# Loads of h spread over slots, first tiles' transposes and first copies moved ahead, dense stream of the forward GLA pass one unit ahead

## The reference

```
h = rmsnorm(x) * norm_g
proj = h @ w_in            # q,k,v and decay gates of the GLA, three z, q,k,v of the attention, cross q, merge gates
o_a = gla_branch(...) * silu(z_a)         # forward and backward scan over the tokens, summed
o_b = diff_attention(...) * silu(z_b);  o_c = memory_cross_attention(...) * silu(z_c)
merged = sum_i sigmoid(gate_i) * (o_i @ w_branch_i)
y = rmsnorm(x + merged @ w_out)
```

## Time and profile before

| | |
|---|---|
| median of three runs | 3385.5 us (3385.05 to 3393.41) |
| profiled execution | 3387.87 us, its span 3386.1 us |
| TensorE busy | 3268.4 us, 97% of the span |
| VectorE, ScalarE, GpSimd busy | 59%, 39%, 32% |
| DMA | 164 GB/s over the span |
| mean granted TensorE clock | 0.985 |

### The profile page before, as it was taken

The page is one execution under the profiler, slowest core; times in us unless marked ns, Lnnn a source line. Parts: engine busy times, 40 slices in busy tenths (PEclk is TensorE's granted clock), DMA queues, the critical chain, the costliest instruction groups (busy, mean ns, idle before and its releaser), DMA issues. The chain is left out here.

```text
span 3386.1 us, 50920 instructions
## 1 busy us (share of the span) xinstructions
PE 3268.4 (97%) x19012; PEld 2552.1 (75%) x19012; DVE 2010.2 (59%) x4623; ACT 1329.7 (39%) x2170; POOL 1097.9 (32%) x511
## 2 busy tenths in 40 slices
PE   7999999998999999999999988999999888999998
PEld 6888888887888888888877765666666566888887
DVE  3322312226667666676667778888888466556654
ACT  3111111114334343444322336666666565333322
POOL 2412313243333333333333325555555433000000
PEclk9999999999999999999999989999999999999999
DMA  6545445465454544544459964122121366667562
GB/s 210 191 147 185 166 153 182 167 216 182 135 191 138 186 149 132 193 137 148 138 168 298 323 209 146 38 78 77 53 63 38 106 236 220 235 225 240 174 219 73
DMA packets 319013, 555.62 MB, mean 164 GB/s; under 512 B 35694, under 2 KB 115438, under 8 KB 318768
## 3 DMA queue, kind: packets, MB, share of 16 engines
q1 hardware_dynamic: 267296, 471.66, 42.9%
q10 hardware_dynamic: 51472, 80.71, 6.6%
HBM read 382.43 MB, written 169.82 MB: 163 GB/s over the span
## 5 line engine op out<-in xcount | busy, mean ns | idle before, releaser
L774 POOL TENSOR_TENSOR glaf_w_lo<-early_raw,glaf_w_hi 128x1024 fp32r<-128x1024 f32 x140 | 342.9, 2450 | 631.0 <-ACT glaf_w_hi L748 629.4
L803 PE MATMUL glaf_dense_acc<-h_hi,glaf_w_hi 128*128 128x512 f32 x1120 | 451.3, 403 | 5.5 <-ACT glaf_dense_out L757 4.1
L803 PE MATMUL glaf_dense_acc<-h_lo,glaf_w_hi 128*128 128x512 f32 x1120 | 439.3, 392 | 0.0
L803 PE MATMUL glaf_dense_acc<-h_hi,glaf_w_lo 128*128 128x512 f32 x1120 | 436.5, 391 | 0.0
L1792 DVE CUSTOM_DVE_ANT_0 front_p<-diff_s_ps,ahead_table 128x512 f32<-128x512 f32 x544 | 347.2, 687 | 72.4 <-PE diff_s_ps L1654 71.6
L555 POOL TENSOR_TENSOR proj_w_lo<-early_raw,proj_w_hi 128x1024 fp32r<-128x1024 f32 x84 | 202.8, 2415 | 481.7 <-DVE proj_w_hi L505 481.7
L1735 ACT ACTIVATE front_p<-front_p,diff_neg_max 128x2048 f32<-128x2048 f32 (+1 forms) x160 | 278.8, 1743 | 7.1 <-DVE diff_neg_max L1800 7.0
L1678 PE MATMUL diff_oT_ps<-diff_aT,diff_v 128*128 128x512 f32 x544 | 272.4, 602 | 4.7 <-ACT diff_aT L1729 4.7
L215 PE MATMUL proj_acc<-h_hi,proj_w_hi 128*128 128x512 f32 x672 | 263.0, 391 | 0.6 <-POOL proj_w_lo L555 0.6
L1653 PE MATMUL diff_s_ps<-ahead_k,ahead_q_high 128*128 128x512 f32 x544 | 244.6, 450 | 18.4 <-PEq L75 8.7
L217 PE MATMUL proj_acc<-h_hi,proj_w_lo 128*128 128x512 f32 x672 | 261.7, 389 | 0.0
(11 more groups left out here) (223 smaller groups left out, 7158.8 us busy)
## 6 DMA issues: line engine op xcount, KB each, us to landing
early_raw<-in_w_zg SPq DMA_DIRECT2D x180, 512.0 KB, 4.2
early_raw<-in_w_stream SPq DMA_DIRECT2D x80, 512.0 KB, 3.6
scratch_zg<-glaf_dense_out SPq DMA_DIRECT2D x140, 256.0 KB, 2.2
items_raw<-in_w_br SPq DMA_DIRECT2D x120, 256.0 KB, 2.9
merge_gate<-scratch_zg SPq DMA_DIRECT2D x120, 256.0 KB, 3.4
scratch_featT<-proj_out ACTq DMA_DIRECT2D x80, 256.0 KB, 2.3
items_br_hi<-scratch_item_hi SPq DMA_DIRECT2D x60, 256.0 KB, 6.1
items_br_lo<-scratch_item_lo SPq DMA_DIRECT2D x60, 256.0 KB, 6.4
```

Of the source, the lines that this page charges most:

```text
L774: pool.tensor_tensor(self.w_lo[:, s], self.raw[:, u % self.RAW], self.w_hi[:, s], ALU.subtract).then_inc(self.lo_split, 1)
L803: done = pe.matmul(self.acc[:, u % self.banks], a, x, start=i == 0, stop=i == self.PER - 1)
```

## The change

Four edits, three of them in the order of instructions and one in the order of DMAs:

- Projection: the transposes of tile 1 stand inside `first_product`, ahead of its low-h matmuls; those of tiles 2 and 3 behind units 0 and 1 instead of 1 and 2. `high(1)` stands ahead of `high_resident(5)`, `high(2)` and `high(3)` behind the copies of units 0 and 1.
- Forward pass: 30 dense matmuls instead of 40 stand ahead of the first sums. `sums` is cast on ScalarE instead of VectorE, and unit 0 is copied out ahead of the first tile's exponentials instead of among them.
- Forward pass: from slot 6 of tile 0 on, `targets` is 24 higher (at most the total). Slot 6 of tile 0 so has 42 matmuls instead of 18, and the last tile's last two slots have none (18 and 6 before).
- Both passes: `load_h` issues one k per slot over eight slots in the forward pass, two per slot over four in the backward, instead of all eight at once. The loads at the start of the forward pass stay in one piece.

```diff
@@ phase_project, ScalarE and TensorE
             high_resident(4)
+            high(1)
             high_resident(5)
...
                 if c == 0 and at < TT - 1:
-                    high(1 + at)
+                    if 2 + at < TT:
+                        high(2 + at)
...
+                transpose(1)
                 pe.wait_ge(lo_ready, 1)
...
-                if c == 0 and at < TT - 1:
-                    transpose(1 + at)
+                if c == 0 and 2 + at < TT:
+                    transpose(2 + at)
@@ Dense
-    def load_h(self, sp, index):
+    def load_h(self, sp, index, pieces):
...
-        if index >= self.buffers:
+        if index >= self.buffers and 0 in pieces:
             sp.wait_ge(self.unit_done, self.first_of[index - self.buffers + 1])
-        for k in range(KT):
+        for k in pieces:
...
-            if u + 1 in self.first_of:
-                index = self.first_of.index(u + 1) - 1 + self.buffers
-                if index < len(self.chunks):
-                    self.load_h(sp, index)
+        for index in range(self.buffers, len(self.chunks)):
+            last = self.first_of[index - self.buffers + 1] - 1
+            first = (slot - [last in ended for ended in self.ended].index(True)) * self.pieces
+            if 0 <= first < KT:
+                self.load_h(sp, index, range(first, first + self.pieces))
@@ phase_gla_forward (pieces=1; phase_gla_backward passes pieces=2)
-        PER, FIRST_PRODUCTS = len(SHARES), 3
+        PER, FIRST_PRODUCTS = len(SHARES), 2
+        AHEAD_FROM, TOTAL = X_SLOTS, len(FORWARD_UNITS) * Dense.PER
+        targets = [t if i < AHEAD_FROM else min(t + Dense.PER, TOTAL) for i, t in enumerate(spread_over(TOTAL, SHARES, N))]
...
+            act.wait_ge(sums_in, 16)
+            act.activation(sums[:, :, :], sums_raw, ACT.Copy).then_inc(sums_ready, 1)
+            dense.copies(act, FIRST_PRODUCTS)
             for j in range(N):
...
-                        dense.copies(act, slot + 1 + d * PAIRS + a)
+                        if slot + 1 + d * PAIRS + a != FIRST_PRODUCTS:
+                            dense.copies(act, slot + 1 + d * PAIRS + a)
...
-            dve.wait_ge(sums_in, 16)
-            dve.tensor_copy(sums[:, :, :], sums_raw).then_inc(sums_ready, 1)
```

More of the change, by code:

```diff
@@ L673, with __init__ @@
     RAW, WEIGHTS, OUTS, PER = Early.RAW, 3, 2, 3 * KT
-    def __init__(self, m, h, early, which, held, hT_hi, hT_lo, w_zg, zg, units, targets, silu, banks):
+    def __init__(self, m, h, early, which, held, hT_hi, hT_lo, w_zg, zg, units, targets, silu, banks, pieces):
         self.dram = hT_hi, hT_lo, w_zg, zg
@@ L678, in __init__ @@
         self.units, self.count, self.buffers, self.targets, self.silu = units, len(units), H_BUFFERS, targets, silu
-        self.held = held
+        self.held, self.pieces = held, pieces
         self.chunks = list(dict.fromkeys(c for c, _ in units))
@@ L725, in begin_transfers @@
         for index in range(self.held, self.buffers):
-            self.load_h(sp, index)
+            self.load_h(sp, index, range(KT))
     def transfers(self, sp, slot):
@@ L828, in phase_gla_forward @@
         SHARES = [10] * X_SLOTS + [18, 30, 18, 18, 18, 6]
-        PER, FIRST_PRODUCTS = len(SHARES), 3
-        dense = Dense(m, h, early, 0, 1, hT_hi, hT_lo, w_zg, zg, FORWARD_UNITS, spread_over(len(FORWARD_UNITS) * Dense.PER, SHARES, N), False, 2)
+        PER, FIRST_PRODUCTS = len(SHARES), 2
+        AHEAD_FROM, TOTAL = X_SLOTS, len(FORWARD_UNITS) * Dense.PER
+        targets = [t if i < AHEAD_FROM else min(t + Dense.PER, TOTAL) for i, t in enumerate(spread_over(TOTAL, SHARES, N))]
+        dense = Dense(m, h, early, 0, 1, hT_hi, hT_lo, w_zg, zg, FORWARD_UNITS, targets, False, 2, 1)
         qk = m.sb("qk", [P, S, 4, P])
@@ L1200, in phase_gla_backward @@
         order = list(range(SEQS[0] // P - 1, -1, -1)) + list(range(N - 1, SEQS[0] // P - 1, -1))
-        dense = Dense(m, h, early, 1, 2, hT_hi, hT_lo, w_zg, zg, BACKWARD_UNITS, spread_over(len(BACKWARD_UNITS) * Dense.PER, [1, 1], N), True, 3)
+        dense = Dense(m, h, early, 1, 2, hT_hi, hT_lo, w_zg, zg, BACKWARD_UNITS, spread_over(len(BACKWARD_UNITS) * Dense.PER, [1, 1], N), True, 3, 2)
         qb = m.sb("qb", [P, L, PAIRS, P])
```

## The result

The changed kernel takes 3363.87 us (median of 4 runs, 3362.45 to 3367.64) where the kernel before, in turn with it on the same chip, takes 3387.51 (3385.05 to 3393.41): the ratio is 0.993, with a 95% interval of 0.9918 to 0.9943. It is 23.6 us faster, and 3362 was forecast. The total agrees; its terms agree less well.

The account below looks back on a forecast made before the run. TensorE was taken as the bound, full in mid forward pass, so only its waits could be won. Terms 9.3 + 8.1 + 1.0 + 0.4 + 5.0 = 23.8 us off 3387.87 give 3364.1; 2.4 lower for the median: 3362, range 3356 to 3371.

Parts of the forecast that it names:

- Projection: Projection: earlier transposes leave one wait of some 1.8 us and bring unit 3's copy to 46.3 from 55.85; 9.3 us.
- if all stays warm: Upper bound of the projection term, with no matmuls at the low clock: 10.3 us.
- Start of the forward pass: Forward pass start: waits of 4.07 and 1.67 us shrink or go, 24 matmuls are issued earlier; 8.1 us (7.3 to 8.7).
- The step that timed VectorE's chain: Forward pass start: VectorE's chain starts 2.2 us earlier and would be done at 800.0.
- h spread in the forward pass: Forward pass: the one wait for `w_lo`, after a block of 16 h DMAs, goes; 1.0 us (0 to 1.0).
- End of the forward pass: Forward pass end: `o_ps` starts 3.25 us later, but backward weights are issued earlier; 0.4 us gained (-1 to +1).
- h spread in the backward pass: Backward pass: `w_lo` waits of 2.58 and 0.6 us and 2.7 of cold matmuls shrink; 5.0 us (0 to 6.2).
- One sign that I had named against this term: Backward pass: the prediction would be wrong if ScalarE's waits for raw weights grew instead of shrinking.
- The rival that the backward waits stay: Backward pass: waits stay or move as the DMA queue hardly drains; term 0 to 1, total 3366 us, chance 0.20.
- that of a late clock: Projection: inserted transposes make the clock rise later; price 3.3 us, total 3365 us, chance 0.10.
- That of the margins at the forward start: Forward pass start: unit 1's copy comes too late and unit 3 stands; 2 to 4 us, total 3365, chance 0.08.
- It does nothing: Projection's wait only moves to tile 3, forward start's credit is all paid at its end; total 3377 us, chance 0.04.

Follow-up runs that it names:

- e7: The changed kernel with the projection edit undone (transposes and high parts back at their old places): 3373.72 us, ratio 0.9966 to the kernel before.
- e4: The changed kernel with the forward pass's dense stream not a unit ahead (old targets): 3361.01 us, ratio 0.993 to the kernel before.
- e2: The changed kernel with the loads of h in one block again in both passes: 3367.29 us, ratio 0.9953 to the kernel before.
- e3: The changed kernel with one unit of backward weights issued ahead of the forward pass's end, the other three behind the backward pass's start: 3359.95 us.
- e5: The changed kernel with the first four backward weight units loaded one by one as raw buffers come free: 3360.43 us, measured again at 3361.08.
- e6: The kernel of e5 with the forward pass's dense stream not a unit ahead: 3359.86 us, ratio 0.9927 to the kernel before.
- e8: The changed kernel with the cast of the sums back on VectorE, unit 0's earlier copy and the shift kept: 3366.35 us, ratio 0.9942 to the kernel before.
- e11: The kernel of e3 with the forward pass's dense stream not a unit ahead: 3364.32 us, ratio 0.9938 to the kernel before.
- e1: The kernel before with the projection edit alone: 3378.32 us, ratio 0.9981 to the kernel before.

## Why the prediction was right, and where it was not

The range of 3356 to 3371 holds the time. By the profiled executions the gain is 25.4 us of span (3386.1 to 3360.7); the terms were to give 23.8. The first backward matmul comes 17.1 us earlier (1737.14 to 1720.09), where 18 to 19 were named.

**Projection, 9.3 forecast, 11.3 measured; right in mechanism.** One wait is left, ended at 32.20 and so near 33 us as said, of 0.85 us and not 1.8, since the square that tile 3 needs ended at 27.6 and not 28.6. The mis-sized part is the price of cold matmuls: half of it behind the first transposes and half behind the wait were in the sum, and neither fell due. Unit 0's copy came at 24.33 (25.2 forecast), unit 3's at 44.62 (46.3). The bound "if all stays warm" was 10.3; the shorter wait adds the last microsecond. e7 shows it in place, 10 to 12 us.

**Start of the forward pass, 8.1 forecast, 8.5 measured; right in size, partly by luck.** Up to the first turn of the scan, that is (811.24 − 796.86) + 24 × 0.227 − 11.3. Both waits are gone. The step that timed VectorE's chain took its length from the kernel before, where two of six products ran beside GpSimd at 3.4 us; in the changed kernel none does, and the chain is 4.4 us shorter than I counted. So TensorE started at 787.94 when the pick had been done for 3.5 us, and of the 24 matmuls issued ahead fewer were needed than I thought: without them e4 waits only 2.00. The forecast named the start as 799.6; less the projection's 11.3 it is 788.3, where TensorE itself got there.

**h spread in the forward pass, 1.0 forecast, about 1.4 measured**, by what the scan gained from its first to its last turn (21.28 − 11.29 − 8.54). e2 gives 0.6 to 1.8.

**End of the forward pass, +0.4 forecast, −4.2 measured; this step was wrong.** Its first half held: `o_ps` waits 1.81 us for VectorE, and the copy of o comes 4.0 us later than before, against 3.25 forecast (1711.63 + 21.28 saved until then, against 1728.89); the o products behind the wait take 3.04 us to the copy instead of 2.33 (2.41 in the second execution; the granted clock from 1710 to 1711 is 0.53 in the first and 1.00 in the second). What failed is "the next phase 2.75 us later" than the last store, together with the weights being issued "some two microseconds before that". A dense stream that ends a unit early also frees SP early: the weights went out 4.2 us ahead of the store of o, 2 MB, and the store landed in 6.2 us instead of 2.0. The phase started 6.69 us after it. e3 and e5 move these bytes and nothing else, and the phase starts 2.5 us after the store again: shown. The five traces in which the 2 MB are issued ahead of the store agree (it lands in 5.0 to 6.8 us), and so do the eight others (2.0 in each). I costed the early weights as a gain and never asked what they lie ahead of. "Without the early load this edit would cost the 3 us": the load took the 3 us and more.

**h spread in the backward pass, 5.0 forecast, 6.7 measured; right about which waits go, too small, and its mechanism right only in part.** The waits that are gone come to 3.5 us (3.2 for `w_lo` and 0.3 just ahead of the longer one), and the cold matmuls behind them to the 2.7 of the forecast: 6.2 in all. What was mis-sized is the 0.9 that I took off for late weights in other units; no such wait of TensorE shows. The 3.8 to 4.8 of e2 prices the spread too low, because e2 also lacks a wait that both kernels have (the rows are from before, after, after and e2):

```profile
1792.10 0.80 PE L1325 MATMUL glab_o_ps<-glab_state,glab_qb 64*128 64x128 f32 x8 [1.87 <-issue]
...
1767.85 3.33 DVE L1394 SCALAR_TENSOR_TENSOR glab_normed_o<-glab_total,glab_stat,glab_gain 128x128 f32<-128x128 f32 x4
...
1774.74 1.12 PE L1333 MATMUL glab_o_ps<-glab_state,glab_qb 64*128 64x128 f32 x8 [1.87 <-issue]
...
1769.74 1.14 DVE L1394 SCALAR_TENSOR_TENSOR glab_normed_o<-glab_total,glab_stat,glab_gain 128x128 f32<-128x128 f32 x4
```

Between the two request groups VectorE clears the state, and TensorE needs it cleared. Ahead of that stand VectorE's four operations L1394. Where they take 3.33 us the clearing comes late, and TensorE stands 1.87 us, with matmuls at a granted clock of 0.50 behind it (1793 to 1796 before, 1776 to 1778 after); in e2 and e4 they take 1.14 and the wait is absent. GpSimd starts a low part 0.8 us behind their start in all four traces; it takes 2.40 us where VectorE is held up and 2.61 where it is not, so a hair decides which of the two waits. The eight executions with the spread and this wait have backward passes of 270.4 to 271.7 us; e4, with the spread and without the wait, has 268.00, and e2, in one block and without it, is 7.2 longer than e4.

One sign that I had named against this term did show. ScalarE's waits for raw weights in the backward pass were to shrink, and grew a little (before, then after):

```profile
ACT glab_w_hi L748 <- DMA early_raw<-in_w_zg: 29.4, 15, 5.1
...
ACT glab_w_hi L752 <- DMA early_raw<-in_w_zg: 30.7, 15, 4.8
```

They were 29.6 in the second execution and 26.7 in e2. The load of the earlier trace rows took 6.6 us from its issue to ScalarE's start; the one that ScalarE waits longest for after the change takes 7.5 (1904.82 to 1912.36). So less data ahead of a load is not what paid. The weights come more evenly: GpSimd's longest gap between two low parts, 14.2 us before (ended at 1924.38), is 9.7 after (ended at 1913.50). That this evenness is what removed the waits is argued, not shown by a run of its own. The rule of the Trainium skill (DMA: Bandwidth & Descriptors, Specifications), by which this term would be an estimated 3, stands further from the 6.7 than the forecast does; its limit of about 358 GB/s, half of what a stack gives two cores, is passed once more by the 373 of the window 1712 to 1715. Nor were the 379 that I took for the ceiling one: e2 moved 415 GB/s from 1850 to 1852.

**The rest, 0 forecast, 1.7 measured**, is within its own spread of 5 us. So the sum of the terms met the total because the projection's and the backward pass's gains (3.7 more than forecast) paid for the change of phase (4.6 less), and the remainder was chance.

The rival that the backward waits stay is refuted by the list of waits, as is that of a late clock by the window of 1.00. That of the margins at the forward start did not occur: unit 1's copy ran from 778.74 to 779.32, and TensorE came to unit 3 near 781. "It does nothing" had its mechanism right at one point only: the credit of the shift is all paid at the end (e4).

The best kernels here are e3, e4, e5 and e6, 3360 to 3361 us. By the traces the front of the program, up to attention, gains 2.3 to 5.5 us over the changed kernel; by the times they cannot be told from it.

## What to carry to other kernels

When work is moved so that an engine's queue ends earlier, list what that queue now issues earlier, and what small transfer it gets in front of. A store that a phase waits for should have no bulk load ahead of it; put the bulk in pieces into the stream before. And an edit that wins at its own place shifts the rest against each other: price what a chain takes by the state in which it will run, not by the state in which it was recorded, and try each part both alone and taken out of the whole.

## What the runs showed of the hardware that was not expected

- A store of 256 KB landed in 2.0 us where no weights, or 0.5 MB of them, had been issued in the four microseconds ahead of it (eight traces), and in 5.0 to 6.8 us where 2 MB of loads had been issued 3.5 to 5.0 us ahead (five traces: after, its second execution, e2, e7, e8). It was issued from another engine's queue (ACT's, the loads from SP's), and that did not protect it.
- VectorE's product of 128x1024 f32 from SBUF takes 1.21 us, and 3.36 to 3.44 when it starts just behind a low part of weights that GpSimd computes in SBUF; a cast of 128x512 took 0.43 us alone and 2.60 beside GpSimd. In e11 GpSimd ends at 784.75 and the product that began at 782.47 ends at 785.84, 1.09 later, about its time alone: it stands rather than shares. That is the rule of the Trainium skill (SBUF — State Buffer, Who interferes with whom): the later of the two waits for the other's whole instruction. The trace agrees, and the forecast had not used it. How many of the six products meet GpSimd (none in the changed kernel, one in e11, two before, three in e1) goes into the wait at the scan's start (0, 4.15, 1.67 and 4.91 us) but does not give it alone: with none it is 0 in the changed kernel and 2.00 in e4, with two 1.67 before and 0.97 in e8, by where TensorE stands.
- Eight transposes and a wait of 0.85 us did not lower the clock in the projection (windows of 1.00 after), nor did the wait of 1.67 at 802.29 before (1.00 from 802 to 806). Waits of 2.70 us in the projection did each time (0.50 from 28 to 31 before; about eight cold matmuls behind each wait in e7), and so did the 1.87 in the backward pass.
